# GpSimd makes the low weight parts of every second convolution tile, and those tiles multiply them last

## The chip, the cores and the metric

The kernel runs on one core of one Trainium2 chip. The time is device microseconds for one execution. A profiled execution shows TensorE (PE, with its weight loads as PEld), VectorE (DVE), ScalarE (ACT), GpSimd (POOL), SyncE (SP) and the DMA engines. Lower is better.

## What is computed

The reference runs two stacked blocks over 256 tokens of width 1024, in float32. The first block joins a Mamba-2 mixer (SSM) and a gated linear recurrence (LRU) and ends in a feed-forward part; the second block is two layers of hybrid attention. The change touches only the input projection of the first block, where the columns for the SSM's convolution are made:

```python
hn = rmsnorm(h, norm1_w[l])
proj = hn @ w_in[l]
gates, z, xbc, dt_raw, lru_x, lru_y = jnp.split(proj, IN_SPLITS, axis=-1)
...
xbc = jax.nn.silu(causal_dwconv(xbc, conv_w, conv_b))
xs, bm, cm = jnp.split(xbc, [SSM_D_INNER, SSM_D_INNER + SSM_BC_DIM], axis=-1)
```

The convolution is causal, four taps deep and separate for each channel. `xbc` has 3072 channels: 2048 for `xs`, 512 for `bm` and 512 for `cm`.

## The kernel before

**Tiles.** All weight matrices are walked as one list of tiles, `TILES`, of at most 128x2048 float32 numbers (1 MB). A column tile is 256 output columns with all 1024 rows, as 8 chunks of 128 rows. The list opens with `dt`, `lx` 0 to 4, `bc` 0 to 3, `xs` 0 and 1, and goes on with `xs` 2, `ly` 0, `gate` 0, `xs` 3, `ly` 1, `gate` 1, `xs` 4 and so on. A tile's place in the list is its index i: `lx` 2 to 4 are tiles 3 to 5, `bc` 0 to 3 are tiles 6 to 9, `xs` 0 to 2 are tiles 10 to 12, `ly` 0, `gate` 0 and `xs` 3 are tiles 13 to 15, `xs` 4 is tile 18 and `xs` 6 is tile 24. Those of `bc` and `xs` are the tiles with a convolution.

**High and low parts.** A product of float32 numbers is made as three products of reduced numbers. ScalarE copies a tile from `raw` to `w_hi` (rounded; line 975 is its one helper for all activations), and then VectorE subtracts, `w_lo = raw - w_hi` (its `tensor_tensor` helper, line 1365). Activations are split the same way into `act_hi` and `act_lo`. TensorE adds w_hi*act_hi, w_hi*act_lo and w_lo*act_hi into a PSUM bank (line 522), so a column tile has 48 matrix products: 2 column chunks by 8 row chunks by 3. `raw`, `w_hi` and `w_lo` have three buffers each.

**Who makes the low part.** `pool_shares()` gives each tile a share in eighths. That share of the columns goes to GpSimd, which subtracts in pieces of `POOL_PIECE` = 512 columns (line 1937, its helper too), and VectorE does the rest. In the first block's input projection the share is 0 everywhere. A share of 8 leaves VectorE nothing.

**The walk.** ScalarE, VectorE and GpSimd go through the tiles with one function, `walk`. At tile i it calls in turn `lead(i)`, which makes the high or low part of tile i+2; `rest` of the tile before; the stages that `stage_order()` put at the middle of tile i; and `evac(i)`, which takes tile i's result from PSUM. For a convolution tile ScalarE's `evac` writes the last tap and the bias (`conv_open`, two activations), VectorE's adds the other three taps (`conv`, six instructions of line 1373 that read a PSUM bank and `xbc` or `lru_u`), and `rest` is a tanh on ScalarE and a product on VectorE. Each engine's queue runs in this order, and semaphores join them.

**The stages around the change.** `gates_ready` (middle of `lx` 2) makes dt and the recurrence's parameter `lam` in a row of dependent small steps, on VectorE and ScalarE. `lru(h)` for the ten heads stands in `lx` 3 to `bc` 3: two small products on TensorE; two tanh, an exp that needs `lam`, a tanh and a square on ScalarE; two products on VectorE that write `lru_ab` and `lru_u`. `dt_cs` (in `bc` 1) makes the cumulative sum `cs` on VectorE, and ScalarE's queue issues its DMA and so waits for it.

**How TensorE waits.** `columns` waits for both parts of a tile and then makes the three products of each chunk together. `columns_low_last` waits for `w_hi`, makes all products with it, and only then waits for `w_lo` and makes the last 16. Before, only tiles with i < `LOW_LAST` = 6 go that way. Both call the stages of the middle after 24 of the tile's 48 products.

**Loads.** SP issues the load of tile i when `w_hi` and `w_lo` of tile i-3 are done, whichever engine made them.

Of the kernel before, what the change touches and what calls it, by code (L numbers as in the profile page):

```python
# [67 lines left out]
LOW_LAST = 6  # L68
# [22 lines left out]
def tile_names():  # L91
# [20 lines left out]
    for l in range(DEPTH_2):  # L112
# [5 lines left out]
        for i in range(NF2 + 2):  # L118
            if i < NF2:
                names.append(("up", NF2 * l + i))  # L120
            if i >= 2:
# [5 lines left out]
T = {name: i for i, name in enumerate(TILES)}  # L127
DOWNS = ("out_ssm", "out_lru", "out", "ffn_out", "out_2", "down")
TOKENS = ("ret_v", "dil_v")

POOL_SHARE = {"out_ssm": 4, "out_lru": 4,
              "ret_k": 5, "ret_q": 5, "ret_v": 5, "ret_g": 5, "dil_k": 7, "dil_q": 7, "dil_v": 8,
              "out_2": 8}
# [41 lines left out]
def pool_shares():  # L175
    shares = [POOL_SHARE.get(name, 0) for name, _ in TILES]
    shares[0] = shares[1] = 0
    for i in range(1, len(TILES)):
        if (TILES[i][0], TILES[i - 1][0]) in (("ffn_gate", "out"), ("qi", "ffn_out"), ("qi", "down"), ("up", "out_2")):
            shares[i + 1] = 8  # L180
    return shares
# [127 lines left out]
def build(nc, w, x_t, x_tok, rows_w, params, consts, consts_2, out_tok):  # L309
    ctx = ExitStack()  # L310
    with ctx:
# [11 lines left out]
        def tick(name):  # L323
            made[name] = made.get(name, 0) + 1
            return sem(GOES_ON.get(name, (name, 0))[0]), 1

        def at(name, n):
            asked[name] = max(asked.get(name, 0), n)
            first, past = GOES_ON.get(name, (name, 0))
            return sem(first), past + n if n > 0 else 0  # L330
# [103 lines left out]
        def head_rows(t, h):  # L434
# [8 lines left out]
        LAST_TILE = {0: ("out", 3), 1: ("ffn_out", NF1 - 1), 2: ("out_2", OUT_ORDER[-1]), 3: ("down", NF2 - 1),  # L443
                     4: ("out_2", 4 + OUT_ORDER[-1])}
        shares = pool_shares()
        shapes, sources = zip(*[tile_source(w, *t) for t in TILES])
        sizes = [k * n for k, n in shapes]
# [61 lines left out]
        def pe_program():  # L509
# [114 lines left out]
            def opening(i, n):  # L624

                tiles = []
                for i2 in (i, i + 1):
                    name, j = TILES[i2]
                    bank = take(high if name == "up" else low, (name, j), freed_by(name, j))
                    tiles.append((i2, bank, range(shapes[i2][1] // P)))  # L630

                def part(tile, half):
                    i2, bank, chunks = tile
                    hi, lo = tile_ready(i2)
                    for m in chunks:
                        for k in range(4 * half, 4 * half + 4):
                            norm_ready(n, k)
                            inst = product(bank[:, m * SEQ:(m + 1) * SEQ], hi[:, k, m * P:(m + 1) * P],
                                           lo[:, k, m * P:(m + 1) * P], act_hi[:, 8 + k, :], act_lo[:, 8 + k, :],
                                           m == 0 and k == 0, k == DC - 1)  # L640
                    if half:
                        inst.then_inc(*tick("tile_used"))

                part(tiles[0], 0)
                turn(n, 1)
                part(tiles[1], 0)
                part(tiles[0], 1)
                stages("after", i)
                part(tiles[1], 1)
                stages("after", i + 1)  # L650

            def token_columns(i, name, j, base, ring):
                bank = take(ring, (name, j), freed_by(name, j))
                hi, lo = tile_ready(i)
                for t in range(TT):
                    if t:
                        stages("mid", i)
                    for k in range(DC):
                        inst = product(bank[:, t * 256:(t + 1) * 256], act_hi[:, base + k, t * P:(t + 1) * P],
                                       act_lo[:, base + k, t * P:(t + 1) * P], hi[:, k, :], lo[:, k, :], k == 0, k == DC - 1)  # L660
                inst.then_inc(*tick("tile_used"))

            def index_key(i, l, base):

                bank = take(low, ("ki", l), freed_by("ki", l))
                hi, lo = tile_ready(i)
                n = HD + IDX_H
                for k in range(DC):
                    inst = product(bank[0:n, 0:SEQ], hi[:, k, :], lo[:, k, :], act_hi[:, base + k, :],
                                   act_lo[:, base + k, :], k == 0, k == DC - 1)  # L670
                inst.then_inc(*tick("tile_used"))
# [44 lines left out]
            def rows(i, name, j):  # L716
                count, ring = ROWS[name]
                whole, n = divmod(OUT_ORDER.index(j % 4) + 4 * (j // 4) if name == "out_2" else j, count)
                first, last = n == 0, n == count - 1
                hi, lo = tile_ready(i)  # L720
                k0 = rows_ready(name, j)
                if name not in ("out_ssm", "out_lru"):
                    return token_rows(i, name, j, whole, first, last, ring, hi, lo, k0)
                for b in range(DC // 2):
                    if first:
                        acc[name, b] = take(ring, (name, whole, b), freed_acc(name, whole, b))
                    bank = acc[name, b]
                    for j2 in range(2):
                        for m in range(2):
                            c0 = (2 * b + m) * P  # L730
                            inst = product(bank[:, m * SEQ:(m + 1) * SEQ], hi[:, j2, c0:c0 + P], lo[:, j2, c0:c0 + P],
                                           act_hi[:, k0 + j2, :], act_lo[:, k0 + j2, :], first and j2 == 0 and m == 0,
                                           last and j2 == 1)
                    if last and b < DC // 2 - 1:
                        inst.then_inc(*tick("acc_done"))
                inst.then_inc(*tick("tile_used"))
# [28 lines left out]
            def mean(name, total, matrix, ring, freed):  # L765
                bank = take(ring, name, freed)
                for m in range(2):
                    inst = mm(bank[:, 0:SEQ], matrix, total[:, m * SEQ:(m + 1) * SEQ], m == 0, m == 1)
                return inst
# [161 lines left out]
            def stages(where, i):  # L931
                for stage, *args in STAGES.get((where, i), ()):
                    if stage in STAGE:
                        STAGE[stage](*args)
# [4 lines left out]
            for i, (name, j) in enumerate(TILES):  # L939
                if i == 1:  # L940
                    pe.wait_ge(*at("n1_total", 1))
                    mean("n1_mean", tmp[0], c["mean_d"], high, at("n1_root", 1)).then_inc(*tick("n1_mean"))
                if i - 1 in first_of:
                    continue
                if i in first_of:
                    opening(i, first_of[i])
                    continue
                if name in DOWNS:
                    rows(i, name, j)
                else:  # L950
                    base = 0 if UNSCALED <= i < T["ffn_gate", 0] else 8
                    ring = high if name == "up" else low
                    if name in TOKENS:
                        token_columns(i, name, j, base, ring)
                    elif name == "ki":
                        index_key(i, j, base)
                    else:
                        (columns_low_last if i < LOW_LAST else columns)(i, name, j, base, ring)
                stages("after", i)

        SELECT = {}
# [973 lines left out]
        def pool_program():  # L1935
# [46 lines left out]
            walk(lead, lambda i, name, j: None, rest, {"norm_split": norm_split, "lru_split": lru_split, "ret": ret})  # L1982

        pe_program()
        act_program()
        vec_program()
# [88 lines left out]
```

## Time and profile before

| | |
|---|---|
| median of 3 runs | 1235.39 us (1231.95 to 1236.85) |
| profiled execution, its own time | 1235.14 us |
| span in that profile | 1233.8 us |
| mean granted TensorE clock | 0.993 of full |
| PE busy | 1191.5 us |
| DVE busy | 754.8 us |
| ACT busy | 676.8 us |
| POOL busy | 347.5 us |

The span is what the engines' instructions cover; 1.34 us of the execution's time lies outside it. Busy time is an average over parts with different limits, so each stretch has to be read by itself: the stretch in question is 49 to 122 us, the tiles from `bc` 0 to `xs` 3. In a view of waits, "A <- B: us, times, longest" says how long A sat idle until B released it.

### The profile page before, as it was taken

What the parts mean: (1) busy time and instruction counts of PE and PEld (TensorE: products, weight loads), DVE (VectorE), ACT (ScalarE), POOL (GpSimd) and SP (SyncE); (2) the same over time, 40 slices, a digit from 0 to 9 for tenths busy, and PEclk for the clock granted to TensorE, in tenths of its full rate; (3) what the DMA queues carried; (4) which work ended last, traced back from release to release, by engine and by line L of the source; (5) the groups of instructions that cost most, each with busy time, mean ns of one, the idle gap of its engine ahead of it and who ended that gap; (6) DMA issues with size and microseconds to landing.
All of it is one profiled execution on the core that took longest, in us unless ns stands there. A gap on an engine that the chain in (4) does not pass through costs nothing.

```text
span 1233.8 us, 20584 instructions
## 1 busy us (share of the span) xinstructions
PE 1191.5 (97%) x8552; PEld 1102.7 (89%) x8552; DVE 754.8 (61%) x1018; ACT 676.8 (55%) x932; POOL 347.5 (28%) x211
## 2 busy tenths in 40 slices
PE   9798999999999999999999899999999989999997
PEld 8798999999998999999998699999899877999996
DVE  7878988677455645554878354544456953544444
ACT  5778776686435443434646864444454387544442
POOL 0000000035821111112475533222225673322221
PEclk9899999999999999999999999999999999999999
DMA  9444756534555655554543346665554533666560
GB/s 298 154 135 140 239 177 199 187 125 169 184 193 203 205 195 182 185 191 138 183 136 127 104 151 202 194 193 182 163 180 146 163 103 107 201 201 191 177 200 35
DMA packets 152444, 210.77 MB, mean 171 GB/s; under 512 B 5504, under 2 KB 132640, under 8 KB 151712
## 3 DMA queue, kind: packets, MB, share of 16 engines
q1 hardware_dynamic: 151584, 205.08, 51.9%
q10 hardware_dynamic: 768, 4.39, 1.0%
q8 instruction: 68, 1.11, 0.4%
q14 instruction: 24, 0.20, 0.0%
HBM read 208.37 MB, written 1.08 MB: 170 GB/s over the span
## 4 chain that ended last, share of the span: by engine, by line
PE 78%; ACT 10%; DVE 8%; issue 2%; POOL 1%; DMA 1%; SPq 0%; ACTq 0%; DVEq 0%
PE bank L522 77%; ACT w_hi L975 2%; ACT tmp L975 2%; DVE w_lo L1365 2%; ACT L975 2%; PE bank L530 1%; DVE xbc L1373 1%; ACT probs_dil L975 1%; DMA raw<-in_w_in 1%; POOL w_lo L1937 1%; DVE work L1369 1%; ACT lru_ab L975 0%; ACT xbc L975 0%; ACT probs_dsa L975 0%; DVE lru_u L1373 0%
## 5 line engine op out<-in xcount | busy, mean ns | idle before, releaser
L522 PE MATMUL bank<-act_hi,w_hi 128*128 128x256 f32 (+1 forms) x2040 | 582.1, 287 | 16.8 <-DVE w_lo L1365 12.5
L522 PE MATMUL bank<-act_lo,w_hi 128*128 128x256 f32 (+1 forms) x2040 | 574.3, 283 | 0.0
L522 PE MATMUL bank<-act_hi,w_lo 128*128 128x256 f32 (+1 forms) x2040 | 564.2, 283 | 0.0
L1365 DVE TENSOR_TENSOR w_lo<-raw,w_hi 128x2048 fp32r<-128x2048 f32 (+4 forms) x174 | 366.3, 2106 | 242.6 <-ACT w_hi L975 242.5
L975 ACT ACTIVATE w_hi<-raw 128x2048 fp32r<-128x2048 f32 (+1 forms) x191 | 360.0, 1885 | 252.7 <-PE bank L522 245.2
L522 PEld LDWEIGHTS bank<-act_hi,w_hi 128*128 128x128 f32 (+1 forms) x2040 | 390.8, 192 | 26.6 <-issue 19.9
L522 PEld LDWEIGHTS bank<-act_lo,w_hi 128*128 128x128 f32 (+1 forms) x2040 | 391.1, 192 | 2.1 <-issue 0.5
L522 PEld LDWEIGHTS bank<-act_hi,w_lo 128*128 128x128 f32 (+1 forms) x2040 | 385.1, 192 | 0.0
L1937 POOL TENSOR_TENSOR w_lo<-raw,w_hi 128x512 fp32r<-128x512 f32 (+1 forms) x146 | 201.1, 1406 | 436.2 <-ACT w_hi L975 436.2
L1937 POOL TENSOR_TENSOR act_lo<-tmp,act_hi 128x512 fp32r<-128x512 f32 x52 | 135.9, 2617 | 431.0 <-ACT act_hi L975 431.0
L522 PE MATMUL bank<-w_hi,act_hi 128*128 128x512 f32 (+1 forms) x536 | 203.0, 379 | 8.3 <-POOL act_lo L1937 5.7
L522 PE MATMUL bank<-w_lo,act_hi 128*128 128x512 f32 (+1 forms) x536 | 200.1, 373 | 0.0
L522 PE MATMUL bank<-w_hi,act_lo 128*128 128x512 f32 (+1 forms) x536 | 199.8, 373 | 0.0
L522 PEld LDWEIGHTS bank<-w_hi,act_hi 128*128 128x128 f32 x536 | 101.7, 190 | 27.9 <-issue 12.1
L522 PEld LDWEIGHTS bank<-w_hi,act_lo 128*128 128x128 f32 x536 | 101.7, 190 | 18.0
L522 PEld LDWEIGHTS bank<-w_lo,act_hi 128*128 128x128 f32 x536 | 101.7, 190 | 15.9 <-issue 0.5
L975 ACT ACTIVATE tmp<-bank 128x512 f32<-128x512 f32 (+1 forms) x61 | 33.7, 566 | 116.5 <-PE bank L522 116.2
L1373 DVE SCALAR_TENSOR_TENSOR tmp<-bank,tmp 128x512 f32<-128x512 f32 x32 | 22.1, 691 | 59.9 <-ACT tmp L975 59.9
L975 ACT ACTIVATE act_hi<-tmp 128x512 fp32r<-128x512 f32 x55 | 34.3, 624 | 22.2 <-DVE tmp L1373 22.1
L975 ACT ACT_TABLE_LOAD x29 | 37.2, 1283 | 1.7 <-PEq L2068 1.2
L1373 DVE SCALAR_TENSOR_TENSOR xbc<-bank,params,xbc 128x255 f32<-128x255 f32 (+2 forms) x72 | 29.1, 474 | 5.9 <-ACT xbc L975 5.9
L975 ACT ACTIVATE probs_dil<-probs_dil,small 128x128 f32<-128x128 f32 x64 | 26.1, 450 | 2.6 <-DVE small L1826 2.1
(232 smaller groups left out, 801.9 us busy)
## 6 DMA issues: line engine op xcount, KB each, us to landing
raw<-in_w_in SPq DMA_DIRECT2D x64, 1024.0 KB, 5.3
raw<-in_w_up SPq DMA_DIRECT2D x32, 1024.0 KB, 5.7
raw<-in_w_down SPq DMA_DIRECT2D x32, 1024.0 KB, 4.9
raw<-in_w_ffn_in SPq DMA_DIRECT2D x22, 1024.0 KB, 5.1
raw<-in_w_out SPq DMA_DIRECT2D x12, 1024.0 KB, 4.9
raw<-in_w_ffn_out SPq DMA_DIRECT2D x11, 1024.0 KB, 4.9
raw<-in_w_out_ssm SPq DMA_DIRECT2D x8, 1024.0 KB, 4.9
raw<-in_w_out_lru SPq DMA_DIRECT2D x5, 1024.0 KB, 4.9
```

Source lines behind the costliest of these rows:

```text
L522: return mm_ops.matmul(out, lhs, rhs, start=start, stop=stop, skip_group_check=True)
L530: return mm_ops.transpose(out, a, c["ident"][0:k, 0:k])
L975: return ops.activation(out, a, func, bias=bias, scale=scale, accum_out=accum)
L1365: return ops.tensor_tensor(out, a, b, op)
L1369: return ops.tensor_scalar(out, a, s1, None, op0)
L1373: return ops.scalar_tensor_tensor(out=out, in0=a, scalar=s, in1=b, op0=op0, op1=op1, accum_out=accum)
L1937: return nc.gpsimd.tensor_tensor(out, a, b, op)
```

## The change

Six tiles get a share of 8, and so have their whole low part made by GpSimd: `bc` 0 and 2, and `xs` 0, 2, 4 and 6 (tiles 6, 8, 10, 12, 18 and 24). The same six tiles go through `columns_low_last` on TensorE. The sizes of pieces, the order of tiles, the stages and the loads are as before.

```diff
+BY_POOL = [("bc", 0), ("bc", 2)] + [("xs", j) for j in (0, 2, 4, 6)]
...
 def pool_shares():
     shares = [POOL_SHARE.get(name, 0) for name, _ in TILES]
     shares[0] = shares[1] = 0
+    for tile in BY_POOL:
+        shares[T[tile]] = 8
...
-                        (columns_low_last if i < LOW_LAST else columns)(i, name, j, base, ring)
+                        (columns_low_last if i < LOW_LAST or (name, j) in BY_POOL else columns)(i, name, j, base, ring)
```

Three lines are added ahead of the code, so line numbers of the changed kernel are higher by 3 (line 1365 is 1368 there). VectorE's queue before, from the end of `gates_ready` on through the convolution of `lx` 2 to `lru(0)` and `lru(1)`; `w_lo` there is the low part of tile 6:

```order
L1370 TENSOR_SCALAR cs_all<-cs_all 32x256
L1370 TENSOR_SCALAR small<-params 128x10
L1365 TENSOR_TENSOR dt<-dt,cs_all 32x256
L1365 TENSOR_TENSOR small<-small 128x10
L1369 TENSOR_SCALAR small<-small 128x10
L1373 SCALAR_TENSOR_TENSOR lru_u<-bank,params,lru_u 128x255 x2
L1373 SCALAR_TENSOR_TENSOR lru_u<-bank,params,lru_u 128x254 x2
L1373 SCALAR_TENSOR_TENSOR lru_u<-bank,params,lru_u 128x253 x2
L1365 TENSOR_TENSOR w_lo<-raw,w_hi 128x2048
L1373 SCALAR_TENSOR_TENSOR lru_ab<-tmp 128x256
L1373 SCALAR_TENSOR_TENSOR lru_u<-tmp,lru_u 128x256
```

The same place of VectorE's queue now:

```order
L1373 TENSOR_SCALAR cs_all<-cs_all 32x256
L1373 TENSOR_SCALAR small<-params 128x10
L1368 TENSOR_TENSOR dt<-dt,cs_all 32x256
L1368 TENSOR_TENSOR small<-small 128x10
L1372 TENSOR_SCALAR small<-small 128x10
L1376 SCALAR_TENSOR_TENSOR lru_u<-bank,params,lru_u 128x255 x2
L1376 SCALAR_TENSOR_TENSOR lru_u<-bank,params,lru_u 128x254 x2
L1376 SCALAR_TENSOR_TENSOR lru_u<-bank,params,lru_u 128x253 x2
L1376 SCALAR_TENSOR_TENSOR lru_ab<-tmp 128x256
L1376 SCALAR_TENSOR_TENSOR lru_u<-tmp,lru_u 128x256
```

The subtraction over 2048 columns is gone from between the convolution and `lru(0)`, and nothing else moved; five more such rows are gone further on.

GpSimd's queue before, from its start on; the first `act_lo` is of the first normalisation (at 24 us), the rows after it belong to `norm_split` and `out_ssm` (from 262 us on):

```order
L1937 ISA
L1937 TENSOR_TENSOR act_lo<-tmp,act_hi 128x512
L1937 TENSOR_TENSOR w_lo<-raw,w_hi 128x512 x2
L1937 TENSOR_TENSOR act_lo<-tmp,act_hi 128x512 x2
L1937 TENSOR_TENSOR w_lo<-raw,w_hi 128x512 x2
```

GpSimd's queue from its start now:

```order
L1940 ISA
L1940 TENSOR_TENSOR act_lo<-tmp,act_hi 128x512
L1940 TENSOR_TENSOR w_lo<-raw,w_hi 128x512 x26
L1940 TENSOR_TENSOR act_lo<-tmp,act_hi 128x512 x2
L1940 TENSOR_TENSOR w_lo<-raw,w_hi 128x512 x2
```

Where 2 pieces stood between the first two `act_lo` there are 26: four for each of the six tiles, ahead of the 2 of `out_ssm` 0.

TensorE's queue before, in tile 6 (`bc` 0), from the last products ahead of its middle to the first behind it; `lru_u,xbc` is `lru(4)` and `lru(5)`:

```order
L522 MATMUL bank<-act_hi,w_hi 128x256
L522 MATMUL bank<-act_lo,w_hi 128x256
L522 MATMUL bank<-act_hi,w_lo 128x256
L522 MATMUL bank<-lru_u,xbc 128x256 x4
L522 MATMUL bank<-act_hi,w_hi 128x256
L522 MATMUL bank<-act_lo,w_hi 128x256
L522 MATMUL bank<-act_hi,w_lo 128x256
```

The same place of TensorE's queue now, on to the end of tile 6 (rows between are more of the same two):

```order
L525 MATMUL bank<-act_hi,w_hi 128x256
L525 MATMUL bank<-act_lo,w_hi 128x256
L525 MATMUL bank<-lru_u,xbc 128x256 x4
L525 MATMUL bank<-act_hi,w_hi 128x256
L525 MATMUL bank<-act_lo,w_hi 128x256
...
L525 MATMUL bank<-act_hi,w_lo 128x256 x16
```

The 16 products with `w_lo` moved to the end of the tile; the stage of the middle stands where it stood, after 24 products.

## Rows read from the trace of the kernel before

**Rows 1.** The page, part 2: GpSimd's busy tenths in 40 slices of 30.8 us.

```profile
POOL 0000000035821111112475533222225673322221
```

**Rows 2.** Waits of PE (us, times, longest): 0 to 240 us, then 122 to 262 us.

```profile
PE bank L522 <- DVE w_lo L1365: 12.3, 7, 5.9
...
PE bank L522 <- DVE w_lo L1365: 1.2, 1, 1.2
```

**Rows 3.** The chain that ended last, 40 to 140 us: start, us, what.

```profile
70.84 2.43 DVE xbc L1373 x6
73.27 2.20 DVE w_lo L1365
...
88.90 0.91 ACT xbc L975 x2
89.92 2.44 DVE xbc L1373 x6
...
119.94 2.21 DVE w_lo L1365
122.28 3.77 PE bank L522 x28
```

**Rows 4.** Timeline of DVE at tile 6 (start us, us, instruction, [idle before <-releaser]).

```profile
49.34 0.28 DVE L1370 TENSOR_SCALAR cs_all<-cs_all 32x256 f32<-32x256 f32 x1
...
50.08 0.15 DVE L1365 TENSOR_TENSOR small<-small 128x10 f32<-128x10 f32 x1
50.26 0.17 DVE L1369 TENSOR_SCALAR small<-small 128x10 f32<-128x10 f32 x1
50.35 2.43 DVE L1373 SCALAR_TENSOR_TENSOR lru_u<-bank,params,lru_u 128x255 f32<-128x255 f32 x6
52.69 2.29 DVE L1365 TENSOR_TENSOR w_lo<-raw,w_hi 128x2048 fp32r<-128x2048 f32 x1
```

**Rows 5.** Timeline of ACT: high part of tile 6, exp of `lru(0)`, high part of tile 10.

```profile
47.20 1.90 ACT L975 ACTIVATE w_hi<-raw 128x2048 fp32r<-128x2048 f32 x1
...
51.35 0.60 ACT L975 ACTIVATE lru_ab<-tmp,small 128x256 f32<-128x256 f32 x1
...
83.29 1.91 ACT L975 ACTIVATE w_hi<-raw 128x2048 fp32r<-128x2048 f32 x1
```

**Rows 6.** Timeline of DVE, 69 to 90 us, at tiles 8 and 10.

```profile
69.85 0.43 DVE L1373 SCALAR_TENSOR_TENSOR lru_ab<-tmp 128x256 f32<-128x256 f32 x1 [1.03 <-ACT tmp L975]
...
85.85 2.29 DVE L1365 TENSOR_TENSOR w_lo<-raw,w_hi 128x2048 fp32r<-128x2048 f32 x1
88.05 0.69 DVE L1373 SCALAR_TENSOR_TENSOR xbc<-tmp,xbc 128x512 f32<-128x512 f32 x1
88.94 0.42 DVE L1373 SCALAR_TENSOR_TENSOR lru_ab<-tmp 128x256 f32<-128x256 f32 x1 [0.20 <-ACT tmp L975]
89.28 0.42 DVE L1373 SCALAR_TENSOR_TENSOR lru_u<-tmp,lru_u 128x256 f32<-128x256 f32 x1
```

**Rows 7.** Timeline of POOL: a whole tile in four pieces; six pieces; four pieces (last of 256).

```profile
386.61 5.04 POOL L1937 TENSOR_TENSOR w_lo<-raw,w_hi 128x512 fp32r<-128x512 f32 x4 [33.98 <-ACT w_hi L975]
...
299.71 11.46 POOL L1937 TENSOR_TENSOR w_lo<-raw,w_hi 128x512 fp32r<-128x512 f32 x6 [1.97 <-ACT w_hi L975]
...
654.14 4.50 POOL L1937 TENSOR_TENSOR w_lo<-raw,w_hi 128x512 fp32r<-128x512 f32 x4 [2.96 <-ACT w_hi L975]
```

**Rows 8.** Timeline of DVE while POOL ran those six and those four pieces.

```profile
300.81 0.68 DVE L1373 SCALAR_TENSOR_TENSOR tmp<-tmp,bank 128x512 f32<-128x512 f32 x1
...
302.52 2.31 DVE L1365 TENSOR_TENSOR w_lo<-raw,w_hi 128x1024 fp32r<-128x1024 f32 x1
304.76 1.79 DVE L1365 TENSOR_TENSOR tmp<-tmp 128x512 f32<-128x512 f32 x1
...
654.78 4.01 DVE L1369 TENSOR_SCALAR work<-score,top 128x128 f32<-128x128 f32 x4
```

**Rows 9.** Windows view behind PE's longest wait: busy times by engine, PEclk, DMA, GB/s.

```profile
57.00:58.00 1.00, 1.00 (x6) 1.00 (x6) 1.00 (x4) 1.00 (x2) 0.00 (x0) 0.50 1.00 341
```

## The prediction

> **What bounds the kernel now.** I read the slices of the page first. GpSimd is idle from its one early instruction to 262 us [rows 1], so the six tiles find its queue empty, and no work stands behind them until 262 us. Next the waits of TensorE: up to 240 us it waits 12.3 us for VectorE's low parts, 7 times, the longest 5.9 us, and of that only 1.2 us falls behind 122 us [rows 2]. So the stretch with something to win ends at 122.28 us, where tile 15 (`xs` 3) starts [rows 3]; from there TensorE has work without a break. Whatever the change does ahead of this point counts only as far as it moves this start.
>
> What sets that start is read from the chain that ended last [rows 3]. It does not run through TensorE before 122 us but through ScalarE and VectorE, each waiting for the other: the convolution on VectorE at 70.84, the low part of tile 9 at 73.27, ScalarE's opening of the next convolution at 88.90, VectorE's convolution at 89.92, and at last the low part of tile 15 at 119.94, with TensorE behind it. The low parts in the chain belong to tiles 9, 14 and 15, which VectorE keeps. The moved ones are not in it: that of tile 6 runs 52.69 to 54.98 [rows 4] and that of tile 10 runs 85.85 to 88.14 [rows 6], both in time in which the chain is on ScalarE. TensorE's waits for moved tiles are a consequence of this chain and not its cause. This is the point on which the forecast rests.
>
> **What is removed.** Six subtractions over 2048 columns, 2.29 us each [rows 4, 6], leave VectorE: 13.7 us of its busy time. On the path they are worth nothing. Behind the one of tile 10, VectorE still waits 0.20 us for ScalarE's `lru(8)` [rows 6], and the product before the convolution of `bc` 0 has waited 1.03 us for ScalarE [rows 6]: cover is there, and more of it with the subtraction gone.
>
> **What moves on TensorE.** In a moved tile 16 products with `w_lo` go behind the other 32. Their number and lengths are the same, so in itself that costs nothing. It lets TensorE start with the high part, for tile 6 at about 49.2 instead of 55.1 us. The gain doesn't last: tile 7 needs its own low part from VectorE, and so on down to tile 15. In tile 6 TensorE will stop at the middle, since `lru(4)` needs the convolution of `lx` 2 (now at 50.35 to 52.8 [rows 4]), and its clock may fall there. At 57 us, behind today's longest wait, the granted clock is 0.50, which is the lower of the two levels (1.2 against 2.4 GHz) [rows 9]. What hides that is tile 7's wait for its low part. Price on the path: 0. SP's loads of tiles 9, 11, 13, 15, 21 and 27 wait for GpSimd's last piece where they waited for VectorE's subtraction. GpSimd's tile takes 5.04 against 2.29 us [rows 4, 7], so some go out about 3 us later. For tile 13 that is near 91 us, while its high part is due behind the convolution of `bc` 3, ten us later. Nothing is queued behind these loads that is due sooner. Also 0.
>
> **What is added.** GpSimd makes 24 pieces of 512 columns. Left alone, four take 5.04 us, 1.26 each [rows 7]. TensorE asks for them 32 products into the tile, so their own length hardly shows. The price is what they do to VectorE. Six pieces took 11.46 us instead of 7.6 [rows 7], and in that stretch VectorE's subtraction over 1024 columns took 2.31 us (half of 2.29 is 1.15), and a 512-column addition 1.79 us [rows 8]. Each is longer by about one piece: instructions of the two engines alternate, one whole piece between two of VectorE. Four `tensor_scalar` took 4.01 us beside four pieces [rows 8], where one over 32x256 alone takes 0.28 [rows 4]; GpSimd lost next to nothing by those (4.50 us for 1792 columns, and 1792/2048 of 5.04 is 4.41). But an instruction that reads a PSUM bank kept its 0.68 us [rows 8]. So steps that read SBUF only wait up to 1.26 us each while pieces are queued; the convolutions, which read a bank, don't.
>
> The rule behind it is in the Trainium skill, SBUF — State Buffer, "Who interferes with whom": GpSimd and VectorE's second port pair are one lock, taken for a whole instruction, by VectorE instructions with two SBUF inputs or in a two-port mode such as `tensor_scalar`. It speaks against this change. The GPSIMD Engine Reference, section 4.1, does too ("Elementwise add/mul/max on a tile": VectorE, GpSimd being about 2x slower); its section 3.1 has 4497 ns for 2048 columns. This trace has 5.04 us in four pieces. With the page's figure the sum below would be about 0.5 us smaller.
>
> Step A, tile 6. Its high part is done at 49.10 (47.20 + 1.90 [rows 5]), so the pieces end near 50.46, 51.72, 52.98 and 54.24. Just then VectorE is in the last steps of `gates_ready`, from 49.34 on: two `tensor_scalar`, two additions and a last `tensor_scalar` that makes `lam`, done at 50.43 [rows 4]. They are short, but each of the first four would wait for the end of a piece, since at least one passes at each end and each pair depends on the one before. The fourth runs at 54.24, and `lam` is ready about 0.35 later, at 54.6. ScalarE's exp of `lru(0)`, at 51.35 now [rows 5], needs it: it moves by 3.3 us. Behind it ScalarE has no idle time up to the convolution of `bc` 0 at 70.84, so the chain moves by 3.3 us. Bounds: at the low end only the two additions are held (`lam` near 52.0 to 52.3) and it is 0.7 to 1.0; at the high end `lam` waits for the whole 5.04 us and all five steps, 3.6. I take 3.3, as the `tensor_scalar` row is the nearest one.
>
> Step B, tile 8. Its pieces lie over the four products of `lru(4)` and `lru(5)`, ahead of the convolution at 70.84 [rows 3]. The last pair is ready at 69.85 [rows 6], when GpSimd is in its last piece. Bounds 0 and 1.3; I take 0.5, as most of the stretch is over.
>
> Step C, tile 10. High part done at 85.20 [rows 5]. Pieces end at 86.5 and 87.8; then the `xbc` product (0.69 [rows 6]) passes, third piece to about 89.5; the first product of `lru(8)`, ready at 88.94 [rows 6], passes; fourth piece to about 91.0; the second product, now at 89.28 [rows 6], passes, and the convolution starts near 91.3 instead of 89.92 [rows 3]. That is 1.4 us. Bounds: 0, and 2.5 for two whole pieces.
>
> Step D, tile 12. In its stretch VectorE has one step without a bank (`xbc`), and ScalarE is in the square root and its table loads, which cover it: 0, at most 0.5.
>
> Step E, tiles 18 and 24. TensorE bounds here and VectorE is ahead, but the masked products that `ssd_val` waits for can meet a piece. VectorE is also rid of 2.29 us just ahead of them. I take 0.1 in all; bounds -0.5 and 1.
>
> Sum: 3.3 + 0.5 + 1.4 + 0 + 0.1 = 5.3 us. The profiled execution's own time is 1235.14, which gives 1240.4; the median shown, 1235.39, lies 0.25 above it, and I write **1240.5**. The bounds add up to 0.2 and 8.9 us.
>
> **The rivals.** *Light stall*: `tensor_scalar` over so few elements isn't held, so A is 0.7 to 1.0; with B and C as above the sum is 2.8, 1238.0 us. For it: the held rows have 128 partitions by 128 and 256 columns, and these have 32 rows or 10 columns. Against it: four of them show the same wait whatever their size.
>
> *Heavy stall* (the other side): the same alternation, but with VectorE losing each meeting at tiles 8 and 10, so that both products of `lru(5)` and of `lru(8)` wait a whole piece: A 3.6, B 1.3, C 2.5, D and E 0.6 together, 8.0 us, 1243.1 us. It decides from B + C = 2.8 on, where the sum passes 6.2 us. For it: in rows 7 and 8 each VectorE step paid nearly a full piece. Against it: GpSimd's stretches end about when those products come due.
>
> *Gain*: VectorE was the bound of this stretch after all, and TensorE runs ahead once it may start with high parts. Then between the longest wait of 5.9 and all 12.3 us [rows 2] come back: 1229 to 1223, with 1226 in the middle. For it: the waits are named "DVE w_lo". Against it: the chain doesn't hold one moved subtraction.
>
> *It does not do what it says*: the order of instructions shows all 24 pieces on GpSimd and six rows fewer on VectorE, so this gets no chance.
>
> **How the numbers follow.** Half a per cent of the median is 6.2 us, about what a measurement of this kernel can tell from no change (the three runs span 4.9 us). Forecast (sum 3.5 to 6.2) 0.45; light stall or less (0 to 3.5) 0.20; heavy stall (over 6.2) 0.29; gain 0.06. So faster by over 0.5% 0.06, within 0.5% 0.65, slower by over 0.5% 0.29. The range from 1234.5 to 1245.5 takes in both stalls, the bounds of the sum and some spread of the runs, and leaves the gain out.
>
> **What would show it.** In the changed profile TensorE starts tile 6 near 49.2 us and stops in its middle. VectorE's last steps of `gates_ready` are spread over 5 us, and ScalarE waits about 3 us for `small` before the exp of `lru(0)`. The convolution of `bc` 0 starts near 74.6, that of `bc` 2 near 95.1, and tile 15 starts near 127.5 instead of 122.28; behind it the distances are as before. GpSimd's pieces of tile 6 take 5.1 to 5.5 us. The forecast is wrong if `lam` comes before 53 us, if the chain has slack between 51 and 70 us, or if tile 15 starts before 122 us.

## The result, and the profile after

| | before | after |
|---|---|---|
| median | 1235.39 us (7 runs, 1231.95 to 1236.85) | 1240.14 us (7 runs, 1238.64 to 1241.74) |
| ratio to before | | 1.0039, 95% interval 1.0029 to 1.0050 |
| profiled execution, its own time | 1235.14 us | 1241.74 us |
| span in that profile | 1233.8 us | 1240.4 us |

The change costs 4.7 us of the medians, 0.39%. That is within the half per cent to which the prediction gave 0.65, and the interval leaves out 1: slower, by less than half a per cent. GpSimd is busy 380.7 us instead of 347.5 and VectorE 754.0 instead of 754.8: 13.7 us of subtractions are gone from VectorE, and 12.9 us have come into its other instructions, which take longer where they meet a piece of GpSimd. Below, such an instruction is called held.

The slices of the page; against [rows 1], GpSimd now works in the slices from 31 to 186 us, the last two for tiles 18 and 24:

```profile
POOL 0122110025931111112465433222216663222221
```

TensorE's waits, 0 to 250 us (us, times, longest). Against [rows 2], the waits for VectorE's low parts halve, and others come in their place; GpSimd is hardly waited for:

```profile
PE bank L525 <- DVE w_lo L1368: 6.1, 5, 2.7
PE bank L525 <- DVE lru_u L1376: 6.0, 2, 4.8
PE bank L525 <- ACT w_hi L978: 2.8, 2, 2.3
...
PE bank L525 <- POOL w_lo L1940: 0.2, 1, 0.2
```

Timeline of GpSimd: the four pieces of tiles 6, 8 and 10 (those of tiles 12, 18 and 24 took 5.50, 5.51 and 5.94 us). As [rows 7], each line is four pieces together:

```profile
49.47 5.22 POOL L1940 TENSOR_TENSOR w_lo<-raw,w_hi 128x512 fp32r<-128x512 f32 x4 [23.73 <-ACT w_hi L978]
68.88 5.40 POOL L1940 TENSOR_TENSOR w_lo<-raw,w_hi 128x512 fp32r<-128x512 f32 x4 [14.19 <-ACT w_hi L978]
89.25 5.65 POOL L1940 TENSOR_TENSOR w_lo<-raw,w_hi 128x512 fp32r<-128x512 f32 x4 [14.96 <-ACT w_hi L978]
```

Timeline of VectorE beside the pieces of tile 6, to be read against [rows 4]. The first step was 0.28 us and is 1.27, the fourth was 0.15 and is 1.22; the fifth begins when GpSimd is done and is as short as before. The convolution of `lx` 2 took 2.43 as before, but here it runs behind the last piece (49.47 + 5.22 = 54.69), so it says nothing yet on whether a step that reads a bank is held:

```profile
49.63 1.27 DVE L1373 TENSOR_SCALAR cs_all<-cs_all 32x256 f32<-32x256 f32 x1
50.83 1.25 DVE L1373 TENSOR_SCALAR small<-params 128x10 f32<-128x10 f32 x1
52.11 1.45 DVE L1368 TENSOR_TENSOR dt<-dt,cs_all 32x256 f32<-32x256 f32 x1
53.49 1.22 DVE L1368 TENSOR_TENSOR small<-small 128x10 f32<-128x10 f32 x1
54.74 0.17 DVE L1372 TENSOR_SCALAR small<-small 128x10 f32<-128x10 f32 x1
54.84 2.43 DVE L1376 SCALAR_TENSOR_TENSOR lru_u<-bank,params,lru_u 128x255 f32<-128x255 f32 x6
```

ScalarE's exp of `lru(0)`, which was at 51.35 [rows 5]:

```profile
54.95 0.60 ACT L978 ACTIVATE lru_ab<-tmp,small 128x256 f32<-128x256 f32 x1 [3.41 <-DVE small L1372]
```

VectorE beside the pieces of tiles 8 and 10, against [rows 6]; the fourth and the last line here are the convolutions of `bc` 0 and `bc` 2, at 70.84 and 89.92 before [rows 3]:

```profile
71.14 0.55 DVE L1376 SCALAR_TENSOR_TENSOR lru_ab<-tmp 128x256 f32<-128x256 f32 x1 [1.60 <-ACT tmp L978]
71.62 1.51 DVE L1376 SCALAR_TENSOR_TENSOR lru_u<-tmp,lru_u 128x256 f32<-128x256 f32 x1
73.44 1.13 DVE L1376 SCALAR_TENSOR_TENSOR lru_ab<-tmp 128x256 f32<-128x256 f32 x1 [0.31 <-ACT tmp L978]
...
74.83 2.42 DVE L1376 SCALAR_TENSOR_TENSOR xbc<-bank,params,xbc 128x255 f32<-128x255 f32 x6
...
90.61 1.70 DVE L1376 SCALAR_TENSOR_TENSOR xbc<-tmp,xbc 128x512 f32<-128x512 f32 x1 [0.70 <-ACT tmp L978]
92.91 0.83 DVE L1376 SCALAR_TENSOR_TENSOR lru_ab<-tmp 128x256 f32<-128x256 f32 x1 [0.60 <-ACT tmp L978]
93.67 1.52 DVE L1376 SCALAR_TENSOR_TENSOR lru_u<-tmp,lru_u 128x256 f32<-128x256 f32 x1
95.11 2.03 DVE L1376 SCALAR_TENSOR_TENSOR xbc<-bank,params,xbc 128x255 f32<-128x255 f32 x5
```

TensorE: the stop in the middle of tile 6, the start of tile 15 (122.28 before, [rows 3]) and the first product of `ssd_val` in tile 18, the first stage that uses the masked products:

```profile
57.41 2.90 PE L525 MATMUL bank<-lru_u,xbc 128*128 128x256 f32 x6 [4.83 <-DVE lru_u L1376]
...
127.44 0.36 PE L525 MATMUL bank<-act_hi,w_hi 128*128 128x256 f32 x1 [1.24 <-DVE w_lo L1368]
...
144.38 0.88 PE L525 MATMUL bank<-tmp,xdt 128*64 128x256 f32 x8 [0.81 <-issue]
```

The chain that ended last, 40 to 145 us, now runs through the small steps of `gates_ready` and through a held product of `lru(8)`, none of which stood in [rows 3] (start, us, what):

```profile
49.63 1.27 DVE cs_all L1373
...
52.11 1.45 DVE dt L1368
...
92.91 0.83 DVE lru_ab L1376
```

**The balance.** This profile runs 0.29 us late before anything has changed (`gates_ready`'s reciprocal is at 46.72, at 46.43 before). Lateness against before, place by place: exp of `lru(0)` 3.60, convolution of `bc` 0 3.99, of `bc` 2 5.19, of `xs` 0 5.16, start of tile 15 5.16, first `ssd_val` 5.39. It stays at 5.4 until about 650 us. Less the 0.29 of the start, the change has cost 5.1 us there. The profiled execution ends 6.6 later, not 5.4: windows of 50 us show a clock of 0.93 at 650 to 700 us (1.00 before) and of 1.00 at 1000 to 1050 us (0.97 before). Read at GpSimd's pieces, the lateness goes from 5.4 near 660 us to 8.2 near 706 and back to 6.6 near 1041. Such steps do not follow the change: over 640 to 700 us the clock is 1.00 in extra_read and 0.97 in bc0_only, over 1000 to 1050 us 1.00 and 0.97, and extra_read, 3.3 us late at 262 us, ends its profiled execution at 1235.26. Before alone, executed 26 times beside the experiments, reached from 1231.86 us at a mean clock of 0.995 to 1237.16 at 0.991. So I compare kernels below by two measures: the ratio of the times, and the lateness at 262 us, where `out_ssm` begins, less the lateness at that reciprocal: 5.10 for after.

### The profile page after: what moved, and what is told of

The parts are those of the page before. It is cut to its first block, busy times and chain, and to the rows that moved or that the text cites. A ratio compares the mean times of both kernels' runs of the same rounds, so it can differ in the third digit from the quotient of the medians.

```text
span 1240.4 us, 20606 instructions
## 1 busy us (share of the span) xinstructions
PE 1197.6 (97%) x8552; PEld 1107.3 (89%) x8552; DVE 754.0 (61%) x1012; ACT 676.7 (55%) x932; POOL 380.7 (31%) x235
## 4 chain that ended last, share of the span: by engine, by line
PE 78%; ACT 9%; DVE 8%; issue 2%; DMA 1%; POOL 1%; SPq 0%; ACTq 0%; DVEq 0%
PE bank L525 76%; ACT w_hi L978 2%; ACT tmp L978 2%; PE bank L533 1%; ACT L978 1%; DVE w_lo L1368 1%; DMA raw<-in_w_in 1%; DVE xbc L1376 1%; ACT probs_dil L978 1%; POOL w_lo L1940 1%; DVE work L1372 1%; ACT lru_ab L978 0%; DVE lru_u L1376 0%; ACT probs_dsa L978 0%; DVE small L1829 0%
## 5 line engine op out<-in xcount | busy, mean ns | idle before, releaser
L525 PE MATMUL bank<-act_hi,w_lo 128*128 128x256 f32 (+1 forms) x2040 | 549.4, 283 | 0.2 <-POOL w_lo L1940 0.2
L1368 DVE TENSOR_TENSOR w_lo<-raw,w_hi 128x2048 fp32r<-128x2048 f32 (+4 forms) x168 | 352.6, 2100 | 242.4 <-ACT w_hi L978 242.3
L525 PEld LDWEIGHTS bank<-act_hi,w_lo 128*128 128x128 f32 (+1 forms) x2040 | 378.3, 192 | 0.4 <-POOL w_lo L1940 0.4
L1940 POOL TENSOR_TENSOR w_lo<-raw,w_hi 128x512 fp32r<-128x512 f32 (+1 forms) x170 | 234.3, 1407 | 409.3 <-ACT w_hi L978 409.3
```

Of the source, the lines that this page charges most:

```text
L525: return mm_ops.matmul(out, lhs, rhs, start=start, stop=stop, skip_group_check=True)
L1368: return ops.tensor_tensor(out, a, b, op)
L1940: return nc.gpsimd.tensor_tensor(out, a, b, op)
```

## The experiments

Each kernel was timed against before on the same chip; "late" is what its profile has lost at 262 us (GpSimd's first piece of `out_ssm`) since the reciprocal near 46.4.

| kernel | median us | before beside it | ratio [95%] | late, us |
|---|---|---|---|---|
| after | 1240.14 | 1235.39 | 1.0039 [1.0029, 1.0050] | 5.10 |
| bc0_only | 1239.57 | 1234.95 | 1.0034 [1.0021, 1.0048] | 3.30 |
| without_bc0 | 1237.48 | 1234.95 | 1.0016 [1.0004, 1.0028] | 1.79 |
| order_only | 1234.93 | 1234.95 | 1.0000 [0.9991, 1.0009] | -0.05 |
| after_lam | 1237.10 | 1234.95 | 1.0018 [1.0005, 1.0030] | 1.74 |
| pieces_128 | 1235.84 | 1235.21 | 1.0011 [1.0000, 1.0021] | 0.56 |
| low_last_16 | 1237.58 | 1235.21 | 1.0019 [1.0009, 1.0029] | 2.22 |
| cs_early | 1230.47 | 1235.21 | 0.9966 [0.9954, 0.9978] | -3.94 |
| cs_low_last | 1233.72 | 1235.21 | 0.9990 [0.9979, 1.0001] | -1.27 |
| extra_read | 1238.48 | 1234.78 | 1.0036 [1.0022, 1.0050] | 3.30 |
| extra_write | 1234.98 | 1234.78 | 1.0000 [0.9990, 1.0009] | -0.02 |
| cs_scans | 1230.05 | 1234.78 | 0.9960 [0.9945, 0.9975] | -5.23 |

**Which tile costs what.** My theory: step A (tile 6) is two thirds of the loss and the rest comes at tiles 8 and 10. The rival: the new order of the products on TensorE is what costs, or hides a gain. Three kernels, edits against after:

```diff
-BY_POOL = [("bc", 0), ("bc", 2)] + [("xs", j) for j in (0, 2, 4, 6)]
+BY_POOL = [("bc", 0)]                                         # bc0_only
+BY_POOL = [("bc", 2)] + [("xs", j) for j in (0, 2, 4, 6)]     # without_bc0
...
-    for tile in BY_POOL:                                      # order_only: these two lines go
-        shares[T[tile]] = 8
```

> Only the first of the six tiles (tile 6, `bc` 0) goes to GpSimd and multiplies its low part last; the other five are as before. Theory (GpSimd's pieces hold the last steps of `gates_ready` and so the exp of `lru(0)`): `lam` about 54.7 us, ScalarE waits 3.4 us for it, tile 15 starts 3.3 to 3.6 us later than before, at about 125.7, and the time is 3.3 us above before (1.0027). Rival 'each moved tile costs its share': a sixth of the loss, 0.8 us. Rival 'the loss is TensorE's own': the middle stop in tile 6 costs nothing at tile 15.

> Five tiles on GpSimd (8, 10, 12, 18, 24), tile 6 stays with VectorE. Theory: what is left of the loss is that of tile 8 (0.4 us), tile 10 (1.2 us) and the masked products behind tile 15 (0.2 us): tile 15 starts 1.6 us later than before, at about 123.9, time 1.8 us above before (1.0015). Rival 'each moved tile costs its share': five sixths of the loss, 4 us.

> The six tiles multiply their low part last on TensorE, but VectorE makes every low part, as before. Theory (the chain of ScalarE and VectorE sets the start of tile 15, which is none of the six): tile 15 starts at 122.3 us as before, time within 0.5 us of before (1.000). Rival 'TensorE gains by starting early': tile 15 starts earlier by some of the 8 us that TensorE waited ahead of tiles 6, 10 and 12, time 2 to 6 us below before.

Measured: tile 6 alone 3.30, all the others 1.79, together 5.09 beside 5.10 for both. The ratios are blunter: 0.34% and 0.16% beside 0.39%, which agree within their intervals. In bc0_only the exp of `lru(0)` is at 54.52 behind a wait of 3.42 us for `small`; in without_bc0 it is at 51.64 and the convolution of `bc` 0 at 71.50. With all low parts back on VectorE and the new order kept, nothing is left: 1.0000 [0.9991, 1.0009]. TensorE then waits 9.1 us for low parts in place of 12.3, and 1.8 us in place of 1.2 for `lru_u`, and tile 15 starts at 122.18. So the order is worth nothing, as a waiting TensorE is not what holds this stretch up.

**Is it the meeting with `gates_ready`?** If tile 6 costs because its pieces meet those five small steps, it is enough to let them pass first. Edit of after, in GpSimd's walk ahead of its wait for the high part:

```diff
+                    if n == T["bc", 0]:
+                        pool.wait_ge(*at("lam", 1))
                     pool.wait_ge(*at("w_hi", n + 1))
```

> The changed kernel, with one wait more: GpSimd begins tile 6 only when `lam` is made. Theory (the loss at tile 6 is the steps of `gates_ready` waiting for pieces): `lam` is back at about 50.5 us, pieces run 50.6 to 56, the exp of `lru(0)` starts at 51.4, and 3.3 us of the loss go: time 1.5 to 2 us above before (1.0015). Rival (the loss at tile 6 comes from TensorE's stop and its clock, or from the low part coming late): nothing is won, 5 us above before.

The pieces begin at 51.07 instead of 49.47, the five steps are back at 0.28, 0.15, 0.41, 0.15 and 0.17 us, exp of `lru(0)` waits no more, and the kernel is 1.74 late, which is what without_bc0 shows (1.79). Starting 1.3 us later on GpSimd (4.08 behind the reciprocal instead of 2.75) ends the stretch 3.4 us sooner.

Two products with two SBUF inputs each, at 53.82 and 55.78 us, are held here (1.49 and 0.97 us instead of 0.42), and cost nothing at 262 us. The convolution of `lx` 2 does run beside pieces (51.07 to 56.46 us) in after_lam, and keeps its length:

```profile
50.91 2.43 DVE L1376 SCALAR_TENSOR_TENSOR lru_u<-bank,params,lru_u 128x255 f32<-128x255 f32 x6
```

**Is it the length of a piece?** In after the held steps start 1.20 to 1.38 us apart, about one piece each (1.27 to 1.44), so a shorter piece should cost less in the same measure. Edit of after, for the six tiles alone:

```diff
-                    for c0 in range(0, cuts[n], POOL_PIECE):
-                        s = slice(c0, min(c0 + POOL_PIECE, cuts[n]))
+                    for c0 in range(0, cuts[n], 128 if TILES[n] in BY_POOL else POOL_PIECE):
+                        s = slice(c0, min(c0 + (128 if TILES[n] in BY_POOL else POOL_PIECE), cuts[n]))
```

> The changed kernel, with pieces of 128 columns instead of 512 for the six tiles (16 pieces a tile). From 1.26 us for 512 columns and 0.73 us for 256, a piece of 128 is put at 0.46 us, 7.4 us a tile. Theory (each step of VectorE that reads SBUF only waits for the end of one piece): the steps of `gates_ready` wait about 0.4 us each instead of 1.2, `lam` is made near 51.8, the exp of `lru(0)` moves by 0.5 us instead of 3.3; at tiles 8 and 10 0.2 and 0.5 us; time about 1.5 us above before (1.0012). Rival (VectorE is held as long as GpSimd works, whatever the piece): tile 6 costs 3.3 us or more, as its 16 pieces take longer in all; 6 us or more above before.

Timeline of GpSimd at tile 6 in pieces_128:

```profile
48.78 7.68 POOL L1940 TENSOR_TENSOR w_lo<-raw,w_hi 128x128 fp32r<-128x128 f32 x16 [23.73 <-ACT w_hi L978]
```

and of VectorE beside it:

```profile
48.94 0.45 DVE L1373 TENSOR_SCALAR cs_all<-cs_all 32x256 f32<-32x256 f32 x1
49.31 0.42 DVE L1373 TENSOR_SCALAR small<-params 128x10 f32<-128x10 f32 x1
49.77 0.64 DVE L1368 TENSOR_TENSOR dt<-dt,cs_all 32x256 f32<-32x256 f32 x1
50.33 0.42 DVE L1368 TENSOR_TENSOR small<-small 128x10 f32<-128x10 f32 x1
50.78 0.39 DVE L1372 TENSOR_SCALAR small<-small 128x10 f32<-128x10 f32 x1
```

Each of the four steps is longer by 0.17 to 0.27 us instead of 1.0 to 1.1; the fifth, which was free, is now held too, by 0.22. GpSimd's tile now takes 7.68 us, and that of tile 10 9.60, of which 2.5 are one piece that met VectorE's low part of tile 11 (92.37 to 94.65 us): GpSimd is held as well. TensorE waits 5.51 us for that tile, and its clock is 0.50 behind the wait (95 to 99 us). But the exp waits only 0.36 us, and the kernel is 0.56 late; by the ratio it is 0.11%, or 1.4 us, with an interval from 0 to 0.21%. That refutes the rival, which asked for 6 us or more. The loss goes with the length of one piece and not with how long GpSimd works.

**Reading or just working?** To tell whether anything moved by the change matters, I left before as it is and gave GpSimd four useless instructions of 512 columns at tile 6 (they write into `z_silu`, which is not in use yet, and VectorE's first `z` waits for them): in one kernel subtractions of constants, which read two operands, in the other `memset`, which reads nothing.

```diff
+                    if n == T["bc", 0]:
+                        pool.wait_ge(sem("consts_arrived"), 16)
+                        pool.wait_ge(*at("w_hi", n + 1))
+                        for q in range(4):
+                            inst = tt(z_silu[:, 2 * q:2 * q + 2, :].rearrange("p k t -> p (k t)"), con[:, 0:512], con[:, 128:640], ALU.subtract)
+                        inst.then_inc(*tick("extra"))
...
+                            inst = nc.gpsimd.memset(z_silu[:, 2 * q:2 * q + 2, :].rearrange("p k t -> p (k t)"), 0.0)
```

> The kernel before, with nothing moved; GpSimd does four extra subtractions of two 512-column stretches of `consts` into the still unused `z_silu`, as soon as the high part of tile 6 is there (work that nobody needs). Theory (the loss at tile 6 is GpSimd's reading beside the steps of `gates_ready`): pieces of 1.26 us, `lam` near 54.7 us, exp of `lru(0)` 3.4 us late, and here the low part of tile 6 is still VectorE's, so the loss is no smaller: 3.3 to 4 us above before (1.003). Rival (the loss comes from reading the same `raw` and `w_hi`, or from the low part's new place): 0.

> As the run before, but GpSimd's four extra instructions only write (memset of 512 columns each). If the two engines meet at reads alone, the additions of `gates_ready` keep their 0.41 and 0.15 us, `lam` stays at 50.4 to 51 us and the time at before (1.000); the two-port `tensor_scalar` may still wait once or twice, at most one piece each, 1 us in all. If any work of GpSimd holds VectorE, it is as with reads, for as long as the four memsets last.

extra_read, on GpSimd and on VectorE:

```profile
49.31 5.15 POOL L1938 TENSOR_TENSOR z_silu<-consts 128x512 f32<-128x512 f32 x4 [23.82 <-ACT w_hi L975]
```

```profile
49.39 1.32 DVE L1370 TENSOR_SCALAR cs_all<-cs_all 32x256 f32<-32x256 f32 x1
50.64 1.22 DVE L1370 TENSOR_SCALAR small<-params 128x10 f32<-128x10 f32 x1
51.89 1.44 DVE L1365 TENSOR_TENSOR dt<-dt,cs_all 32x256 f32<-32x256 f32 x1
53.26 1.22 DVE L1365 TENSOR_TENSOR small<-small 128x10 f32<-128x10 f32 x1
```

extra_write, on GpSimd and on VectorE:

```profile
49.10 2.09 POOL L1953 MEMSET z_silu<- 128x512 f32 x4 [23.77 <-ACT w_hi L975]
```

```profile
49.22 0.55 DVE L1370 TENSOR_SCALAR cs_all<-cs_all 32x256 f32<-32x256 f32 x1
49.70 0.56 DVE L1370 TENSOR_SCALAR small<-params 128x10 f32<-128x10 f32 x1
50.29 0.41 DVE L1365 TENSOR_TENSOR dt<-dt,cs_all 32x256 f32<-32x256 f32 x1
50.63 0.15 DVE L1365 TENSOR_TENSOR small<-small 128x10 f32<-128x10 f32 x1
50.82 0.40 DVE L1369 TENSOR_SCALAR small<-small 128x10 f32<-128x10 f32 x1
```

With nothing moved off VectorE and nothing reordered on TensorE, four subtractions cost what tile 6 costs: 3.30 late like bc0_only, and a ratio of 1.0036 beside 1.0034. Four `memset` cost nothing at 262 us. That by itself proves little, as they are over in 2.09 us: the three `tensor_scalar` grow by 0.27, 0.41 and 0.23 us, and before had 0.9 us to spare between `lam` (50.43) and the exp (51.35), which takes that up. What separates reading from writing is the two additions: they run beside the last `memset`s and stay at 0.41 and 0.15. The Trainium skill, SBUF — State Buffer, "Who interferes with whom", says so: a VectorE instruction with two SBUF inputs contends with a GpSimd instruction that reads SBUF, and not with one that only writes. These two traces agree.

**Could the stretch go faster at all?** The prediction gave the *Gain* rival 6 in 100 because the chain holds no moved subtraction. Three kernels test this from the other side, edits against before: two edits, and both together (cs_low_last). low_last_16 lets every tile up to 15 start with its high part, so that TensorE stands free of the low parts everywhere. cs_early shortens the chain itself: in `bc` 1, VectorE makes `cs` behind the low part of tile 9, and ScalarE's queue waits for it to issue the DMA; in cs_early it is made in `bc` 0, between `lru(4)` and `lru(5)`, where VectorE waits for ScalarE [rows 6]. The DMA stays where it is.

```diff
-LOW_LAST = 6
+LOW_LAST = 16                                                   # low_last_16
...
-    put("mid", ("bc", 0), ("lru", 4), ("lru", 5))
+    put("mid", ("bc", 0), ("lru", 4), ("cs", ), ("lru", 5))     # cs_early
-            STAGE = {"gates_ready": gates_ready, "dt_cs": dt_cs, "dt_turn": dt_turn, "lru": lru,
+            STAGE = {"gates_ready": gates_ready, "cs": dt_cs, "dt_turn": dt_turn, "lru": lru,
```

> The kernel before, with the order of TensorE alone changed for all tiles up to 15: each multiplies its low part last. Every low part is made where it was. Theory (tile 15 starts when its low part is there, and the high parts of tiles 14 and 15 are there at 112.0 and 116.6 us): TensorE starts tile 14 at about 112, tile 15 at 117.8 and ends it at about 125.3 instead of 129.8; of these 4.5 us 2 to 4.5 are kept, since the next tiles' high parts are made only behind it: time 1231 to 1233. Rival (the chain of ScalarE and VectorE sets everything behind tile 15 too): nothing kept, 1235.

> The kernel before, with VectorE's cumulative sum `cs` made between its parts of `lru(4)` and `lru(5)` (where it sits idle 1 us) instead of behind the low part of tile 9; ScalarE's queue still issues its DMA in `bc` 1. Theory (the chain of the two engines sets the start of tile 15): ScalarE's wait of 3.8 us for `cs` goes, the whole chain behind it moves up, and tile 15 starts at about 118.6 instead of 122.28: time 3.5 us below before, 1231.9 (0.997). Rival (TensorE or VectorE's load bounds the stretch): tile 15 as before, 1235.

> The kernel before with both: `cs` made early and all tiles up to 15 with their low part last. If both gains are of the same chain but at different places they add up: tile 15 ends 6 to 8 us earlier than before, time 1228 to 1230. If either fills the same idle time as the other, it is no better than the better one alone.

cs_early: ScalarE's first tanh of `lru(6)`, in before and then in cs_early:

```profile
77.77 0.84 ACT L975 ACTIVATE tmp<-bank,params 128x256 f32<-128x256 f32 x2 [3.84 <-DVE cs L1537]
```

```profile
73.81 0.82 ACT L975 ACTIVATE tmp<-bank,params 128x256 f32<-128x256 f32 x2
```

The wait of 3.84 us is gone, the convolution of `bc` 1 is at 79.53 (83.50 before), tile 15 starts at 118.32 (122.28), and the gain lasts to the end (0.9966). Here a shorter chain of ScalarE and VectorE made the kernel faster one for one.

low_last_16 is a miss. TensorE is ahead in tiles 14 and 15, as I had wanted, and yet the kernel is 2.22 us late. Before, at tile 18, on TensorE and on VectorE:

```profile
138.99 0.88 PE L522 MATMUL bank<-tmp,xdt 128*64 128x256 f32 x8 [0.56 <-issue]
```

```profile
137.88 1.01 DVE L1365 TENSOR_TENSOR tmp<-tmp,cb_mask 128x384 f32<-128x384 f32 x2
```

low_last_16 in the same place, and its windows (busy us of PE, PEld, DVE, ACT, POOL, then the granted clock):

```profile
139.60 1.55 PE L522 MATMUL bank<-tmp,xdt 128*64 128x256 f32 x8 [4.45 <-issue]
```

```profile
138.48 1.02 DVE L1365 TENSOR_TENSOR tmp<-tmp,cb_mask 128x384 f32<-128x384 f32 x2
```

```profile
136.00:138.00 2.00, 0.00 (x0) 0.00 (x0) 2.00 (x2) 2.00 (x6) 0.00 (x0) 0.96 0.11 38
138.00:140.00 2.00, 0.40 (x2) 0.33 (x4) 2.00 (x4) 2.00 (x4) 0.00 (x0) 0.50 0.31 47
140.00:142.00 2.00, 2.00 (x12) 1.46 (x9) 1.15 (x2) 2.00 (x4) 0.00 (x0) 0.50 1.06 368
142.00:146.00 4.00, 4.00 (x26) 4.00 (x26) 3.86 (x6) 1.83 (x6) 0.00 (x0) 0.67 0.55 142
```

The wait put down to "issue" is one for VectorE's masked products `tmp<-tmp,cb_mask`. They don't come sooner than before (this profile starts 0.61 late, and 138.48 less 0.61 is 137.87): VectorE works without a break from 110.89 on. So what TensorE gains in tiles 14 and 15 it waits here in one piece, 4.45 us. In this stop the granted clock falls to 0.50, the lower of its two levels (1.2 of 2.4 GHz), and the first products behind it run at it: eight take 1.55 us instead of 0.88. The first `ssd_val` itself is at 139.60 less 0.61, 138.99, the same as before to the hundredth; the second is at 148.58 less 0.61, 147.97, where before had 145.75. So all 2.22 us go between these two, where the lower clock stands. cs_low_last, for which I had hoped that both gains add up (1228 to 1230), is a miss too: 1233.72, with the same wait (4.4 us), losing 2.7 of the 3.94 us of cs_early.

That gave the last kernel. The ten `lru_scan` stages (a scan of 0.69 and an addition of 0.40 to 0.42 us each) stand ahead of the masked products on VectorE; cs_scans is cs_early with each pair moved behind them:

```diff
-    for j in range(5):
-        put("mid", ("xs", 2 + j), ("lru_scan", 2 * j), ("lru_scan", 2 * j + 1))
+    for j in range(5):
+        put("mid", ("ly", j), ("lru_scan", 2 * j), ("lru_scan", 2 * j + 1))
```

> The kernel before with `cs` made early, and the two scans of each `lru_scan` pair moved on VectorE from the middle of `xs` to the middle of the next `ly`, behind the masked products. Theory, mended by the run with all low parts last (VectorE is full from 110 us on, and the first masked products, at 138.8 us before, set TensorE's first `ssd_val`): each of the two marks has one pair of scans less ahead of it, 2.1 us; tile 15 starts at about 116.2 instead of 118.3, the first `ssd_val` at about 132.9 instead of 135.0: time 2 us below the kernel with `cs` alone, 1228.5 (0.995 of before). Rival (TensorE takes over as the bound at once): as with `cs` alone, 1230.5.

Timeline of TensorE, the first and the second `ssd_val` of cs_scans:

```profile
132.69 0.88 PE L522 MATMUL bank<-tmp,xdt 128*64 128x256 f32 x8
...
140.28 0.88 PE L522 MATMUL bank<-tmp,xdt 128*64 128x256 f32 x8 [0.77 <-DVE tmp L1365]
```

The first comes 2.33 us sooner than in cs_early (135.02; 2.13 less the difference of the starts), and no longer behind a wait. But now the second waits 0.77 us for VectorE, and by 262 us 1.29 us are left (5.23 against 3.94 early). In time it is 0.9960 [0.9945, 0.9975], which is not to be told from cs_early's 0.9966: the 1228.5 that I expected did not come, and the median of 1230.05 is nearer the rival's 1230.5. Both beat both kernels, by 4 to 5 us against before.

## Why the prediction was right

The forecast was 1240.5 and the median 1240.14; the mechanism and its size were both as worked out. That all five steps came within 0.2 us of the values taken is partly luck: B and E were picks inside their bounds (0 to 1.3, and -0.5 to 1), not worked out. By its steps:

- **What bounds the kernel.** Right in what decides: the chain is one of ScalarE and VectorE, and low parts taken from VectorE bring nothing. order_only (1.0000) shows it for TensorE's side, extra_read for VectorE's: it costs 3.30 with all subtractions left on VectorE, bc0_only 3.30 with one gone. Wrong in one sentence: "from there TensorE has work without a break". The stretch doesn't end at tile 15 but at the first `ssd_val` at 138.99, where a wait of 0.56 us named "issue" stood. low_last_16 shows that the masked products bind there. This did no harm to the forecast, as the change moves both by nearly the same (5.16 and 5.39), but it is why I missed low_last_16.
- **Step A**, 3.3 us expected (bounds 0.7 and 3.6): 3.60 - 0.29 = 3.31. The first four of the five steps met the pieces one by one and the fifth came behind them, as told. The *Light stall* is refuted by the rows of 10 columns (0.15 to 1.25 us). The rule of the Trainium skill, SBUF — State Buffer, "Who interferes with whom", has the same order: it lets steps with two SBUF inputs and `tensor_scalar` contend with GpSimd, and not those with one SBUF input outside the two-port modes. The traces agree: 0.15 to 1.22 and 0.15 to 1.25 us for the first two kinds here, 2.43 us for the convolution beside pieces in after_lam.
- **Step B**, 0.5 expected: 3.99 - 3.60 = 0.39. Two products were held (1.51 and 1.13 us instead of about 0.42), and the wait for ScalarE ahead of the second covered part of it.
- **Step C**, 1.4 expected: 5.19 - 3.99 = 1.20. Three products were held (1.70, 0.83 and 1.52 us instead of 0.69, 0.42 and 0.42), the first behind a cover. With that B + C is 1.59, below the 2.8 of the *Heavy stall*.
- **Step D**, 0 expected: -0.03, though the `xbc` product took 1.74 us; the wait for ScalarE behind it is 1.83 us.
- **Step E**, 0.1 expected: 5.39 - 5.16 = 0.23, at tile 18, where the wait named "issue" grew from 0.56 to 0.81 (the masked products took 1.48 us beside pieces instead of 1.01).
- **Sum** 5.3 expected, 5.1 found up to 262 us. The median moved by 4.7; the steps of the clock between the kernel's parts (2.8 and 1.6 us in this profile) are larger than the difference. The *Gain* asked for 1223 to 1229 and a start of tile 15 before 122 us; it was at 127.44.
- **Moved on TensorE**, 0 expected: the stop in the middle of tile 6 came (4.83 us), the clock fell as well (0.50 in the window 57 to 60 us), and tile 7 began its products at 64.57 behind a wait of 0.21 us for its low part, so VectorE still set its start, though narrowly. pieces_128 adds that a wait of 5.51 us for GpSimd's part of tile 10 costs at most the 0.56 that it is late in all.
- **What was to be seen.** Tile 6 starts at 49.44 (49.2), the convolutions of `bc` 0 and 2 at 74.83 and 95.11 (74.6 and 95.1), tile 15 at 127.44 (127.5), GpSimd's first tile takes 5.22 us (5.1 to 5.5).

## What to carry to other kernels

Before work is given to GpSimd, look not at how idle it is but at what VectorE does in those microseconds: while GpSimd works through reading instructions, each of VectorE's steps that has two SBUF inputs or is a `tensor_scalar` waited here for about one GpSimd instruction, however small the step, and a row of dependent small steps paid once for each. Where that lies on the chain, start GpSimd's work behind it (after_lam won back 3.4 us of the 5.1 by waiting), or cut it fine (pieces of 128 columns won back 4.5 us by the lateness, about 3.5 by the ratios, and cost GpSimd half as much time again). Where ScalarE or another engine leaves a gap behind the held step, it costs nothing. And before an engine's waits are removed, follow the chain to the next place where that engine waits, under whatever name: a wait that is only moved can come back in one piece and bring the slow clock with it.

## What the runs showed of the hardware

- The costs on the chain add up to within 0.1 us: tile 6 alone 3.30, the others 1.79, both 5.10, and a useless read in place of tile 6's work 3.30. I had expected the held steps to depend more on where a piece happens to end.
- Four times finer pieces make a tile of GpSimd dearer by a half: 16 of 128 columns took 7.68 us, where four of 512 took 5.22. The shortest piece took 1.26 us with 512 columns, 0.73 with 256 and 0.45 with 128, so a piece has a part that doesn't shrink with it, by an estimate from these some 0.2 us.
- The two engines hold each other: in pieces_128 a 128-column piece that met a VectorE subtraction of 2048 columns took 2.5 us instead of 0.45.
- Before, 26 times on one chip, took 1231.86 to 1237.16 us at mean granted clocks of 0.995 to 0.991. The profiles of the different kernels show where such differences come in: in steps of 1.6 and 2.8 us at places far behind the edit, with a clock of 0.93 in one and 1.00 in the other over 50 us. A loss of 5 us is clearest where it is measured ahead of them.
